# Two-layer transformer with routed experts on one core: the last block's rows are added to the tokens chunk by chunk

## The reference

```python
for layer in range(DEPTH):                                # 2
    h = modulate(rmsnorm(x, norm_attn[layer]), sh_a, sc_a)
    y = attention(h)             # layer 1 also makes its keys and values from x
    x = x + g_a[:, None, :] * y
    h = modulate(rmsnorm(x, norm_ffn[layer]), sh_f, sc_f)
    y = hier_moe(h)              # top 2 of 32 experts, weighted, added per token
    x = x + g_f[:, None, :] * y
return x

def rmsnorm(t, g):
    return t * lax.rsqrt(jnp.mean(t * t, axis=-1, keepdims=True) + EPS) * g
```

## Time and profile before

| | us |
|---|---|
| median of 3 runs | 1744.58 |
| runs | 1741.25 to 1745.68 |
| the profiled execution | 1743.2 |
| its span, first to last instruction | 1741.4 |
| TensorE busy | 1624.5 (93%) |
| VectorE busy | 653.8 (38%) |
| ScalarE busy | 373.2 (21%) |
| GpSimd busy | 71.2 (4%) |
| mean granted TensorE clock | 0.973 of full speed |

### The profile page before, as it was taken

The page is one execution under the profiler, slowest core; times in us unless marked ns, Lnnn a source line. Parts: engine busy times, 40 slices in busy tenths (PEclk is TensorE's granted clock), DMA queues, the critical chain, the costliest instruction groups (busy, mean ns, idle before and its releaser), DMA issues.

```text
span 1741.4 us, 17712 instructions
## 1 busy us (share of the span) xinstructions
PE 1624.5 (93%) x6682; PEld 700.8 (40%) x6682; DVE 653.8 (38%) x1382; ACT 373.2 (21%) x919; POOL 71.2 (4%) x91
## 2 busy tenths in 40 slices
PE   5989998988999997998899999998889999979996
PEld 2435454462343332332344455444453333323332
DVE  2676665351323322323476122224531322322331
ACT  3023444231001010010410334333320101001000
POOL 1100000100000000000000000001000000000000
PEclk9999999999999998999999999998999999989999
DMA  9983823179999999999977021033389999999997
GB/s 353 372 308 100 288 97 146 52 285 389 430 426 426 425 428 427 427 428 419 364 240 243 1 97 49 1 124 123 141 365 420 427 423 427 429 426 426 428 427 293
DMA packets 109478, 526.64 MB, mean 302 GB/s; under 512 B 7921, under 2 KB 49122, under 8 KB 84682
## 3 DMA queue, kind: packets, MB, share of 16 engines
q1 hardware_dynamic: 80080, 486.56, 68.7%
q10 hardware_dynamic: 21322, 19.63, 3.6%
q0 software_dynamic: 7984, 19.22, 3.0%
HBM read 524.44 MB, written 8.48 MB: 306 GB/s over the span
## 4 chain that ended last, share of the span: by engine, by line
PE 81%; DMA 9%; DVE 5%; issue 2%; ACT 1%; SPq 1%; ACTq 0%; DVEq 0%
PE psum L2259 20%; PE psum L2290 11%; PE psum L2305 10%; PE psum L2016 10%; PE psum L1816 7%; PE psum L1988 4%; PE psum L1871 3%; DMA XN<-in_moe_w_up_dram 3%; DMA ring<-in_moe_w_up_dram 3%; DMA HT<-in_moe_w_down_dram 2%; PE psum L2237 2%; DVE W L1154 2%; DMA ring<-in_ada_w_dram 1%; PE psum L2123 1%; PE psum L1999 1%
## 5 line engine op out<-in xcount | busy, mean ns | idle before, releaser
L2259 PE MATMUL psum<-ring,V 128*32 128x512 f32 (+2 forms) x1376 | 352.3, 617 | 17.3 <-issue 9.4
L2305 PE MATMUL psum<-V,W 128*128 128x512 f32 x448 | 218.6, 613 | 3.6 <-DVE X L1606 1.1
L1606 DVE TENSOR_TENSOR X<-X,psum 128x512 f32<-128x512 f32 x224 | 153.7, 687 | 109.4 <-PE psum L2305 109.0
L2259 PEld LDWEIGHTS psum<-ring,V 128*32 128x32 f32 (+2 forms) x1376 | 115.9, 134 | 192.9 <-issue 192.6
L2290 PE MATMUL psum<-ring,V 128*64 128x512 f32 (+2 forms) x608 | 181.0, 596 | 0.8 <-issue 0.8
L1154 DVE SCALAR_TENSOR_TENSOR W<-ring,cact,W 128x512 f32<-128x512 f32 (+1 forms) x224 | 138.4, 618 | 7.7
L1046 ACT ACTIVATE V<-psum,modall,scls 128x128 f32<-128x128 f32 x216 | 81.2, 456 | 272.5 <-PE psum L2237 255.6
L2305 PEld LDWEIGHTS psum<-V,W 128*128 128x128 f32 x448 | 72.4, 188 | 148.5 <-DVE X L1606 85.3
L1055 ACT ACTIVATE V<-psum 128x512 f32<-128x512 f32 x28 | 16.7, 597 | 510.3 <-PE psum L2268 399.2
L2259 PE MATMUL psum<-HT,V 128*64 128x512 f32 (+2 forms) x224 | 102.4, 611 | 17.9 <-DMA XN<-in_moe_w_up_dram 17.5
L1816 PE MATMUL psum<-HT,ring 128*128 128x512 f32 x256 | 116.8, 602 | 0.0
(11 more groups left out here) (334 smaller groups left out, 1836.6 us busy)
## 6 DMA issues: line engine op xcount, KB each, us to landing
ring<-in_moe_w_up_dram SPq DMA_DIRECT2D x45, 2048.0 KB, 25.6
ring<-in_moe_w_gate_dram SPq DMA_DIRECT2D x41, 2048.0 KB, 25.3
ring<-in_moe_w_down_dram SPq DMA_DIRECT2D x38, 2048.0 KB, 25.4
ring<-in_ada_w_dram SPq DMA_DIRECT2D x16, 2048.0 KB, 15.8
HT<-in_moe_w_gate_dram SPq DMA_DIRECT2D x10, 2048.0 KB, 23.8
XN<-in_moe_w_up_dram SPq DMA_DIRECT2D x8, 2048.0 KB, 23.8
ring<-in_ada_w_dram ACTq DMA_DIRECT2D x16, 1024.0 KB, 5.2
T<-in_moe_w_up_dram SPq DMA_DIRECT2D x7, 2048.0 KB, 27.4
```

Source lines behind the costliest of these rows:

```text
L1606: return dve.tensor_tensor(x3[:, c, cols], x3[:, c, cols], sum_bank(p, hf, c), ALU.add)
L2259: ins = pe.matmul(bank[2 + 2 * i + b][half * w:(half + 1) * w, :], V[:, col:col + w], slot3(x)[:, k, :], start=(k == 0), stop=(k == KC - 1))
L2305: pe.matmul(sum_bank(p, hf, c), PICK[p % 2][:, c * P:(c + 1) * P], Y[:, hf * HALF:(hf + 1) * HALF], start=True, stop=True).then_inc(s["sum ...
```

## The change

The order of the last eight sums and adds is turned from half by half to chunk by chunk, in both layers, on TensorE and VectorE. The banks of the sums are renamed so that chunks 0 and 1 use banks 4 to 7 and chunks 2 and 3 use banks 0 to 3. Between the layers ScalarE squares both halves of a chunk and takes its root before it goes to the next chunk; VectorE makes each chunk's mean of the first half by an operation of its own right behind the chunk's adds; and the normalising of chunk 0 and the reciprocal of chunk 1 move ahead of the adds of chunk 3. The stores' code is the same, but `x_new` is now signalled after every second add.

```diff
-                return bank[((2, 3, 4, 5), (0, 1, 6, 7))[hf][c]]
+                return bank[((4, 5, 2, 3), (6, 7, 0, 1))[hf][c]]
...
                 def root_of_halves(c):
-                    act.wait_ge(*s["rms_arg"](1))
+                    act.wait_ge(*s["rms_arg"](c + 1))
...
                     for c in range(TC):
                         act.wait_ge(*sm[0]["summed"](2 * TC * (NB - 1) + c + 1))
-                        ins = act.activation(V[:, HALF * c:HALF * (c + 1)], x3[:, c, 0:HALF], ACT.Square, accum_out=small[:, c:c + 1])
-                    ins.then_inc(half_sq, 1)
-                    for c in range(TC):
+                        act.activation(V[:, HALF * c:HALF * (c + 1)], x3[:, c, 0:HALF], ACT.Square,
+                                       accum_out=small[:, c:c + 1]).then_inc(half_sq, 1)
                         act.wait_ge(*sm[0]["x_new"](c + 1))
                         act.activation(V[:, HALF * (TC + c):HALF * (TC + c + 1)], x3[:, c, HALF:D], ACT.Square,
                                        accum_out=small[:, 40 + c:41 + c]).then_inc(s["ss_ready"].sem, 1)
-                        if c == 0:
-                            root_of_halves(0)
-                    for c in range(1, TC):
                         root_of_halves(c)
...
-                    dve.wait_ge(*s["sum_pe"](2 * TC * p + TC * hf + c + 1))
+                    dve.wait_ge(*s["sum_pe"](2 * TC * p + (TC * hf + c if p < NB - 1 else 2 * c + hf) + 1))
...
+                n1 = sm[1]
                 for c in range(TC):
                     add_sum(NB - 1, 0, c).then_inc(s["summed"].sem, 1)
-                for c in range(TC):
                     add_sum(NB - 1, 1, c).then_inc(s["x_new"].sem, 1)
                     dve.wait_ge(*s["summed"](2 * TC * (NB - 1) + c + 1))
                     dve.wait_ge(*s["x_new"](c + 1))
-                    if l == 0 and c == 1:
-                        dve.wait_ge(half_sq, 1)
-                        dve.tensor_scalar(small[:, 4:8], small[:, 0:4], 1.0 / D, EPS, ALU.mult, ALU.add).then_inc(sm[1]["rms_arg"].sem, 1)
+                    if l == 0:
+                        dve.wait_ge(half_sq, c + 1)
+                        dve.tensor_scalar(small[:, 4 + c:5 + c], small[:, c:c + 1], 1.0 / D, EPS, ALU.mult, ALU.add).then_inc(n1["rms_arg"].sem, 1)
+                    if l == 0 and c == 2:
+                        normalised(n1["rms_root"], n1["xn_ready"], 0, eights=True)
+                        dve.wait_ge(*n1["rms_root"](2))
+                        dve.reciprocal(small[:, 13:14], small[:, 9:10]).then_inc(odd_scale, 1)
                 if l == 0:
-                    n1 = sm[1]
-
-                    normalised(n1["rms_root"], n1["xn_ready"], 0, eights=True)
-                    dve.wait_ge(*n1["rms_root"](2))
-                    dve.reciprocal(small[:, 13:14], small[:, 9:10]).then_inc(odd_scale, 1)
                     normalised(n1["rms_root"], n1["xn_ready"], 2, eights=True)
                     normalised(n1["rms_root"], n1["xn_ready"], 3, eights=True)
...
-                token_sums(NB - 1)
+                pe.wait_ge(*s["picks"](NB))
+                for c in range(TC):
+                    for hf in range(2):
+                        pe.wait_ge(*s["y_evac"](2 * (NB - 1) + hf + 1))
+                        pe.matmul(sum_bank(NB - 1, hf, c), PICK[(NB - 1) % 2][:, c * P:(c + 1) * P], Y[:, hf * HALF:(hf + 1) * HALF],
+                                  start=True, stop=True).then_inc(s["sum_pe"].sem, 1)
```

## The result

The changed kernel is slower by a little: 1746.86 us median (1745.52 to 1750.15, 12 runs) against 1744.37 (1741.25 to 1746.43, 12 runs), ratio 1.0018 with a 95% interval of 1.001 to 1.0026. A second set gave 1.001 (1.0002 to 1.0019). The forecast was 1745.1 in a range of 1741.3 to 1748.5, and within 0.3%. The profiled execution took 1746.93, its span 1745.1.

A forecast was written before the change was run, and what follows sets the result against it. It took VectorE and ScalarE to bound layer 0's end and the store queue layer 1's tail; +1.6 us at the boundary and -1.1 at the tail gave +0.5, a median of 1745.1 us, range 1741.3 to 1748.5.

The forecast's parts named there:

- What bounds each place: End of layer 0 is set by VectorE and ScalarE, the tail of layer 1 by the store queue.
- The tail: End of layer 1: stores no longer queue, -1.2 us, with 0.1 added for a wait in front: -1.1 us.
- the row of 2.7: Layer 1's quickest store, 2.7 us from issue to landing, taken for the last store instead of 3.9.
- the 3.2: Layer 1's end: skill-based estimate of 3.2 us for a lone 512 KB store, making the gain 0.7, not 1.2.
- The 0.1 for the second sum's wait: Layer 1's end: the second sum waits for the second scaled half of the block's rows, 0.1 us, bounds 0 to 0.3.
- The gap behind the short operation: End of layer 0, VectorE: an add starts 0.31 us after a short operation, giving 2.04 us per chunk.
- the boundary is cheap: Rival, chance 0.26: gap of 0.04 at layer 0's end, cost 0.4 to 0.8 us, total 1744.1; sign: pairs 1.7 apart.
- ScalarE's chunk last behind all squares: End of layer 0: ScalarE's scaling of chunk 1 waits for all squares and roots; first copy 1.6 us later.
- The clock: Rival, chance 0.22: first projection matmuls after layer 0 run at half clock, losing 1.6 us more, total 1746.7.
- the prediction's own test: Sign of a lowered clock at the layer boundary: a granted clock row of 0.50 after 861.
- the wait of 2.64: TensorE's wait at layer 0's end, cited as followed by clock 0.50, agreeing with the skill on half rate after waits.

The follow-up runs named there:

- tail_only: Kernel before with chunk by chunk only at the end of layer 1: 1742.24 us against 1744.0, ratio 0.9989; a second set gave 0.9993.
- front_only: Kernel before with chunk by chunk only at the end of layer 0, stores as before: 1747.63 us against 1744.0, ratio 1.0026.
- norm_late: Changed kernel with chunk 0's scaling and chunk 1's reciprocal put behind chunk 3's adds again: 1743.16 us median, ratio 0.9998 to the kernel before.
- after_look1: A further single profile of the changed kernel, nothing altered: second projection unit 24.45 us after layer 0's last scaled rows.
- before_look1: A further single profile of the kernel before, nothing altered: second projection unit 25.23 us after layer 0's last scaled rows.
- after_warm: Changed kernel plus four unused matmuls in TensorE's idle time at the layer boundary: mean 1743.15 us, ratio 0.9997 to the kernel before.

## Why the prediction was right or wrong

The range and "within 0.3%" held; the small loss is larger than forecast, and it came out by other terms, so that part of the hit is luck.

**What bounds each place: right.** The boundary is on the chain by ScalarE's and VectorE's chunks, the tail by the stores. tail_only and front_only split the effect accordingly.

**The tail: right, -1.1 forecast, -1.36 in the profile, -1.3 ± 0.5 in time.** Each store lands in 2.6 us; the row of 2.7 was the right one to take, and the 3.2 worked out from the Trainium skill (DMA: Bandwidth & Descriptors, section on the anatomy of one DMA), whose figures are for the GpSimd path, was too long for a store issued by SyncE. The 0.1 for the second sum's wait was nothing with the last down product at full clock (7.10 us for the sixteen passes) and about right with it at the low one (7.23).

**The gap behind the short operation: wrong.** The walk took 0.31 from one row and built a pitch of 2.04 us per chunk on it. In the changed kernel the adds follow at once (849.48, 849.58). This is the term that was mis-sized: the direct cost is 0.56, not 1.6. It lies between the 0.4 and 0.8 of the rival "the boundary is cheap" (chance 0.26), and the pairs stood 1.75 and 1.80 apart, which the prediction had named as that rival's sign. The last add is 1.05 later, not 2.1. The row's own label, "issue", said that nothing known caused that gap, and it turned up again at the same add and not behind the same kind of instruction. I made a rule of one instance. Why that add starts late stays open.

**ScalarE's chunk last behind all squares: right in place, too large.** The chain goes through chunk 3's squares, the root and L795, which starts 0.58 later, forecast 1.6. norm_late puts most of this on chunk 0's early scaling.

**The clock: a rival at 0.22 that came true in part.** The first profile shows its mechanism as written: the second low stretch reaches into the first projection and costs 0.98 there, forecast 1.6 for it. By the prediction's own test (a row of 0.50 after 861) it was there. Not as written is that the order decides it: after_look1 has the new order without it, before_look1 the old order with it. And two rivals that were priced as alternatives, cheap boundary and low clock, came together. That the measured 1746.86 lies beside the 1746.7 of the low clock confirms nothing, since that sum had 1.6 + 1.6 where the profile has 0.56 + 0.98.

On the page TensorE: Matmul & The Clock Gate of the Trainium skill, section on HAM oscillation, the prediction said that the trace agrees, "0.50 behind the wait of 2.64". That was misread: the four transposes directly behind that wait took 0.66 us at a granted clock of 1.00, and the 0.50 came behind them. In the changed kernel the four behind a wait of 2.29 did run at half rate (857.68, 1.11 us), so the traces agree with the page in one of the two. after_warm shows that work put into the wait cures it.

**The sum.** Direct 0.56, stores -1.36, clock at the boundary 0 to 1.0: between -0.8 and +0.2. Measured is 2.6 ± 0.3 by the means. after_warm, whose boundary is as short as before, should lie at the stores' -1.4 and is at -0.7 ± 0.6; tail_only agrees with its -1.36; front_only at +3.8 ± 0.5 and the changed kernel both lie 2 to 3 us over theirs. Both have 3 to 4 us more of lost clock than before. Shown is that the excess goes when chunk 0's early scaling is undone (norm_late) or TensorE is kept busy at the boundary (after_warm). Not shown is where in the execution all of it sits: of five profiles with the new boundary four place 0.8 to 1.05 us of clock there and one none. Behind it, up to the first expert product of layer 1, these five took 1.0 ± 0.6 us longer than the five with the old boundary or nearly so, which is not clear of noise. Why a half microsecond at the boundary goes with 2 to 3 us more stays open, and with it whether executions with a still longer low stretch there are what the timed runs contain.

## What to carry to other kernels

Work moved ahead of the last chunk on an in-order engine makes the last chunk late (here the last add ended 1.28 us later with chunk 0's scaling ahead of it than with it behind, by norm_late), and its consumers with it; an early first chunk is worth nothing if the next stage needs all. Finishing chunk by chunk pays where a queue of stores stands behind it: look whether the transfers pile up, and count the landing of a lone one (2.6 us here, 3.9 for the last of a queue, 1.3 ± 0.5 us in the total). A delay of half a microsecond in front of TensorE can cost more than itself by its clock, and a few idle matmuls tell whether it does. They are a test and no cure-all: in the new order they took off 3.6 ± 0.6 us, in the old order nothing that could be measured, though the profile was 0.56 shorter.

## What the runs showed that was not expected

The granted clock of one kernel differs between executions at the same instruction: with the same first copy at 14.29 us the clock was down for 3.4 us in one execution of the kernel before and for 6.8 in another, and the second projection unit moved by 1.3 us. Away from the boundary too the time varies: the stretch from the second projection unit to the first expert product of layer 1 took 406.3 to 409.5 us over the ten profiles without extra work at the boundary. One profile against one profile is therefore, by an estimate from these 3 us, good to about 2 us in this kernel, and the split by place is worth more than the difference of the spans.
